# RG-LRU gate matmuls split into two 64-row halves of the array, in a hybrid RG-LRU / HGRN2 decoder layer on one Trainium2 core

## The reference

```python
xb = x.reshape(B, L, N_BLK_A, BLK_A)                       # 8 blocks of 64 channels
r = sigmoid(einsum('blnc,ncd->blnd', xb, wa).reshape(B, L, D_A) + ba)
i = sigmoid(einsum('blnc,ncd->blnd', xb, wx).reshape(B, L, D_A) + bx)
log_a = -C_RGLRU * softplus(-lam) * r
a = exp(log_a)
u = sqrt(maximum(-expm1(2.0 * log_a), 0.0)) * (i * x)
h = associative_scan over tokens of (a, u)                 # h[t] = a[t] * h[t-1] + u[t]
ya = h * silu(ga)
```

## Time and profile before

| | |
|---|---|
| time before, median of 3 runs | 1014.89 us (1014.86 to 1016.26) |
| the profiled execution: its own time, its span | 1015.58 us, 1013.8 us |
| PE busy | 965.2 us, 95% of the span |
| DVE, ACT, POOL busy | 585.0, 429.9, 161.9 us |
| mean granted TensorE clock | 0.984 of full |
| gate matmuls (L509), 128 records | 32.5 us busy, 399 ns mean |

### The profile page before, as it was taken

The page is one execution under the profiler, slowest core; times in us unless marked ns, Lnnn a source line. Parts: engine busy times, 40 slices in busy tenths (PEclk is TensorE's granted clock), DMA queues, the critical chain, the costliest instruction groups (busy, mean ns, idle before and its releaser), DMA issues.

```text
span 1013.8 us, 20053 instructions
## 1 busy us (share of the span) xinstructions
PE 965.2 (95%) x7447; PEld 710.2 (70%) x7502; DVE 585.0 (58%) x1652; ACT 429.9 (42%) x810; POOL 161.9 (16%) x214
## 2 busy tenths in 40 slices
PE   5799968999999999999999999999999999999987
PEld 2567856579766977587757976697659775887554
DVE  2455786446763666357643775466636763477445
ACT  2535476134732374136513471337413651346321
POOL 4000036111120113011201112011201130111112
PEclk9999988999999999999999999999999999999998
DMA  9985211100110011001100011001101010100413
GB/s 313 324 289 167 84 42 45 60 20 3 42 63 0 21 41 63 0 21 42 52 11 21 0 42 63 0 21 41 63 0 41 0 51 1 43 1 25 118 43 112
DMA packets 46590, 60.62 MB, mean 60 GB/s; under 512 B 2748, under 2 KB 40208, under 8 KB 46524
## 3 DMA queue, kind: packets, MB, share of 16 engines
q1 hardware_dynamic: 46524, 59.86, 17.8%
HBM read 48.90 MB, written 10.95 MB: 59 GB/s over the span
## 4 chain that ended last, share of the span: by engine, by line
PE 88%; DVE 5%; DMA 2%; issue 2%; ACT 2%; SPq 1%; DVEq 0%; ACTq 0%
PE ring L392 66%; PE lev L466 7%; PE aux L509 3%; PE okv L493 1%; PE lev L471 1%; PE okv L495 1%; PE okv L494 1%; PE lev L464 1%; DMA woh<-in_ada_w_dram 1%; DMA work<-in_w_in_dram 1%; PE okv L817 1%; PE aux L443 1%; PE aux L479 1%; PE aux L430 1%; PE okv L430 1%
## 5 line engine op out<-in xcount | busy, mean ns | idle before, releaser
L392 PE MATMUL ring<-hnh,wih 128*128 128x256 bf16 (+1 forms) x1152 | 289.4, 262 | 2.6 <-DVE hnl L1281 2.2
L392 PE MATMUL ring<-hnl,wih 128*128 128x256 f16 (+1 forms) x1152 | 289.6, 262 | 0.0
L392 PE MATMUL ring<-hnh,wil 128*128 128x256 bf16 (+1 forms) x1152 | 289.6, 262 | 0.0
L392 PE MATMUL ring<-woh,work 128*128 128x512 f16 x512 | 162.3, 379 | 1.6
L392 PEld LDWEIGHTS ring<-hnh,wih 128*128 128x128 f16 x1152 | 111.8, 99 | 15.1 <-issue 2.2
L1173 DVE TENSOR_TENSOR qq<-qq,gg 128x256 f32<-128x256 f32 x96 | 42.8, 446 | 133.6 <-PE lev L466 95.8
L392 PEld LDWEIGHTS ring<-hnl,wih 128*128 128x128 f16 x1152 | 109.9, 98 | 12.2
L392 PEld LDWEIGHTS ring<-hnh,wil 128*128 128x128 bf16 x1152 | 110.0, 98 | 11.9
L392 PE MATMUL ring<-wih,hnh 128*128 128x512 f16 (+1 forms) x264 | 101.2, 383 | 4.0 <-ACT kk L857 4.0
L392 PE MATMUL ring<-wih,hnl 128*128 128x512 f16 (+1 forms) x264 | 101.1, 383 | 1.4 <-issue 0.2
L1595 POOL TENSOR_TENSOR kk<-kk,cols 128x256 f32<-128x256 f32 x32 | 29.3, 935 | 410.7 <-ACT kk L857 410.7
(11 more groups left out here) (313 smaller groups left out, 1573.5 us busy)
## 6 DMA issues: line engine op xcount, KB each, us to landing
xin<-in_x_prompt_dram SPq DMA_DIRECT2D x16, 512.0 KB, 3.3
work<-in_x_prompt_dram SPq DMA_DIRECT2D x16, 512.0 KB, 4.1
out_dram<-work SPq DMA_DIRECT2D x16, 512.0 KB, 2.6
work<-in_ada_w_dram SPq DMA_DIRECT2D x4, 1024.0 KB, 10.4
woh<-in_ada_w_dram SPq DMA_DIRECT2D x4, 1024.0 KB, 11.8
work<-in_w_in_dram SPq DMA_DIRECT2D x4, 1024.0 KB, 8.5
woh<-in_w_in_dram SPq DMA_DIRECT2D x4, 1024.0 KB, 10.2
wol<-in_w_in_dram SPq DMA_DIRECT2D x4, 1024.0 KB, 9.5
```

Source lines behind the costliest of these rows:

```text
L392: last = mm(out, a(k), b(k), start=start and k == ks[0] and j == 0, stop=stop and k == ks[-1] and j == 2)
```

## The change

`wg` becomes `[128, 4, 128]`: for each channel tile, rows 0 to 63 hold `[wa | wx]` of the even block (columns 0 to 63 the r block, 64 to 127 the i block), rows 64 to 127 hold `[wx | wa]` of the odd block. There are no zeros left, so the memset on POOL and the waits for it go. `gates(n, p)` issues 4 matmuls as before, but each contracts over 64 rows only: half 0 writes `aux[0]`, half 1 writes `aux[1]`, and each result holds 64 channels of r and 64 channels of i. r comes out on its own partitions, i on the other half's. `gates_out` therefore needs 8 sigmoids of 64 partitions x 256 in place of 4 of 128 x 256, each behind one common signal `gates_done`. `r_sig` and `i_sig` count 8 per body.

Waits on PE move with it: both banks are written from the first matmul on, so `gates(n, p)` waits for `kt_sb` ahead of all four; `turn_y` waits for all sigmoids at once, and so does `turn_x`; the first projection of the next body waits for the first r sigmoid of pair 1 (`r_sig.at(n - 1, 5)`) where it waited for all i sigmoids.

```diff
-        wg = sb("wg", [P, 2, CT, P])
+        wg = sb("wg", [P, CT, P])
...
-        gr_ps, gi_ps = Signal("gr_ps", 2), Signal("gi_ps", 2)
+        gates_done = Signal("gates_done", 2)
...
-        r_sig, i_sig, a_exp, th_ok = (Signal(s, 4) for s in ("r_sig", "i_sig", "a_exp", "th_ok"))
+        r_sig, i_sig = Signal("r_sig", 8), Signal("i_sig", 8)
+        a_exp, th_ok = Signal("a_exp", 4), Signal("th_ok", 4)
...
                 if i == 6:
-                    sp.wait_ge(zeroed, 1)
                     for w, src in ((0, rg_wa), (1, rg_wx)):
                         for odd in range(2):
                             v = src[0].rearrange("(t two) c d -> two c t d", two=2)[odd]
-                            sp.dma_start(wg[64 * odd:64 * odd + 64, w, :, 64 * odd:64 * odd + 64], v).then_inc(wg_ld, 16)
+                            co = 64 * (w ^ odd)
+                            sp.dma_start(wg[64 * odd:64 * odd + 64, :, co:co + 64], v).then_inc(wg_ld, 16)
...
                 if j == 0:
                     pe.wait_ge(yb_ok.sem, yb_ok.at(n, 8))
-                    pe.wait_ge(r_sig.sem, r_sig.at(n, 4))
-                else:
-                    pe.wait_ge(i_sig.sem, i_sig.at(n, 4))
+                    pe.wait_ge(r_sig.sem, r_sig.at(n, 8))
+                    pe.wait_ge(i_sig.sem, i_sig.at(n, 8))
...
             def gates(n, p):
                 pe.wait_ge(cvc.sem, cvc.at(n, 8 * p + 8))
-                for w, s in ((0, gr_ps), (1, gi_ps)):
-                    if p == 0 and w == 0:
-                        if not isinstance(n, int) or n > 0:
-                            pe.wait_ge(ytl.sem, ytl.at(n - 1, 2))
-                    elif w == 1:
-                        pe.wait_ge(kt_sb.sem, kt_sb.at(n, p + 1))
-                    elif not (isinstance(n, int) and n == BODIES - 1):
-                        pe.wait_ge(hn_lo.sem, hn_lo.at(n + 1, 2))
-                    for c in range(2):
-                        last = mm(aux[(1 + w + p) % 2][:, T * c:T * c + T], wg[:, w, 2 * p + c, :], xc[:, c, :],
+                if p == 0:
+                    if not isinstance(n, int) or n > 0:
+                        pe.wait_ge(ytl.sem, ytl.at(n - 1, 2))
+                elif not (isinstance(n, int) and n == BODIES - 1):
+                    pe.wait_ge(hn_lo.sem, hn_lo.at(n + 1, 2))
+                pe.wait_ge(kt_sb.sem, kt_sb.at(n, p + 1))
+                for c in range(2):
+                    for half in range(2):
+                        rows = slice(64 * half, 64 * half + 64)
+                        last = mm(aux[half][:, T * c:T * c + T], wg[rows, 2 * p + c, :], xc[rows, c, :],
                                   start=True, stop=True)
-                    last.then_inc(s.sem, 1)
+                last.then_inc(gates_done.sem, 1)
...
                 weights(1)
                 if not first:
-                    pe.wait_ge(i_sig.sem, i_sig.at(n - 1, 4))
+                    pe.wait_ge(r_sig.sem, r_sig.at(n - 1, 5))
                 project(ring[0], FR, 0, n)
...
                 level(n, 1, 6)
-                pe.wait_ge(r_sig.sem, r_sig.at(n, 2))
+                pe.wait_ge(r_sig.sem, r_sig.at(n, 4))
+                pe.wait_ge(i_sig.sem, i_sig.at(n, 4))
                 if not last_body:
                     turn_x(n + 1, 0)
-                    pe.wait_ge(i_sig.sem, i_sig.at(n, 2))
                     turn_x(n + 1, 1)
...
-            pe.wait_ge(i_sig.sem, i_sig.at(n - 1, 4))
+            pe.wait_ge(i_sig.sem, i_sig.at(n - 1, 8))
...
-            for w in range(2):
-                for c in range(CT):
-                    o = TD * CT * w + TD * c
-                    last = mm(lev[1][:, o:o + TD], wg[:, w, c, :], xcd[:, TD * c:TD * c + TD], start=True, stop=True)
+            pe.wait_ge(dv("gp_sb"), 1)
+            for c in range(CT):
+                for half, bank in ((0, lev[1]), (1, okv[0])):
+                    rows = slice(64 * half, 64 * half + 64)
+                    last = mm(bank[:, TD * c:TD * c + TD], wg[rows, c, :], xcd[rows, TD * c:TD * c + TD],
+                              start=True, stop=True)
             last.then_inc(dv("gates_ps"), 1)
...
-                act.wait_ge(gr_ps.sem, gr_ps.at(n, p + 1))
+                act.wait_ge(gates_done.sem, gates_done.at(n, p + 1))
                 act.wait_ge(iu.sem, iu.at(n, p))
                 for c in range(2):
-                    A(rr[:, c, :], aux[(1 + p) % 2][:, T * c:T * c + T], ACT.Sigmoid,
-                      bias=pcol("ba", 2 * p + c)).then_inc(r_sig.sem, 1)
-                act.wait_ge(gi_ps.sem, gi_ps.at(n, p + 1))
+                    for half in range(2):
+                        at = slice(64 * half, 64 * half + 64)
+                        A(rr[at, c, :], aux[half][at, T * c:T * c + T], ACT.Sigmoid,
+                          bias=pcol("ba", 2 * p + c)[at, :]).then_inc(r_sig.sem, 1)
                 act.wait_ge(scan.sem, scan.at(n, 2 * p))
                 for c in range(2):
-                    A(ii[:, c, :], aux[p][:, T * c:T * c + T], ACT.Sigmoid, bias=pcol("bx", 2 * p + c)).then_inc(i_sig.sem, 1)
+                    for half in range(2):
+                        at, of = slice(64 * half, 64 * half + 64), slice(64 - 64 * half, 128 - 64 * half)
+                        A(ii[at, c, :], aux[half][of, T * c:T * c + T], ACT.Sigmoid,
+                          bias=pcol("bx", 2 * p + c)[at, :]).then_inc(i_sig.sem, 1)
```

More of the change, by code:

```diff
@@ L727, in _ @@
             pe.wait_ge(wg_ld, 64)
-            pe.wait_ge(zeroed, 3)
+            pe.wait_ge(zeroed, 2)
             pe.wait_ge(carry_zero, 2)
@@ L904, in gates_out @@
             def gates_out(n, p):
-                act.wait_ge(gr_ps.sem, gr_ps.at(n, p + 1))
+                act.wait_ge(gates_done.sem, gates_done.at(n, p + 1))
                 act.wait_ge(iu.sem, iu.at(n, p))
                 for c in range(2):
-                    A(rr[:, c, :], aux[(1 + p) % 2][:, T * c:T * c + T], ACT.Sigmoid,
-                      bias=pcol("ba", 2 * p + c)).then_inc(r_sig.sem, 1)
-                act.wait_ge(gi_ps.sem, gi_ps.at(n, p + 1))
+                    for half in range(2):
+                        at = slice(64 * half, 64 * half + 64)
+                        A(rr[at, c, :], aux[half][at, T * c:T * c + T], ACT.Sigmoid,
+                          bias=pcol("ba", 2 * p + c)[at, :]).then_inc(r_sig.sem, 1)
                 act.wait_ge(scan.sem, scan.at(n, 2 * p))
                 for c in range(2):
-                    A(ii[:, c, :], aux[p][:, T * c:T * c + T], ACT.Sigmoid, bias=pcol("bx", 2 * p + c)).then_inc(i_sig.sem, 1)
+                    for half in range(2):
+                        at, of = slice(64 * half, 64 * half + 64), slice(64 - 64 * half, 128 - 64 * half)
+                        A(ii[at, c, :], aux[half][of, T * c:T * c + T], ACT.Sigmoid,
+                          bias=pcol("bx", 2 * p + c)[at, :]).then_inc(i_sig.sem, 1)
             def decay(n, p):
-                act.wait_ge(r_sig.sem, r_sig.at(n, 2 * p + 2))
+                act.wait_ge(r_sig.sem, r_sig.at(n, 4 * p + 4))
                 for c in range(2):
@@ L1087, in _ @@
                 for c in range(CT):
-                    o = W4 * w + TD * c
-                    A(dst[:, TD * c:TD * c + TD], lev[1][:, o:o + TD], ACT.Sigmoid, bias=pcol(bias, c)).then_inc(dv("ri_d"), 1)
-            act.wait_ge(dv("ri_d"), 2 * CT)
+                    for half, bank in ((0, lev[1]), (1, okv[0])):
+                        at = slice(64 * half, 64 * half + 64)
+                        of = at if w == 0 else slice(64 - 64 * half, 128 - 64 * half)
+                        A(dst[at, TD * c:TD * c + TD], bank[of, TD * c:TD * c + TD], ACT.Sigmoid,
+                          bias=pcol(bias, c)[at, :]).then_inc(dv("ri_d"), 1)
+            act.wait_ge(dv("ri_d"), 4 * CT)
             for c in range(CT):
@@ L1445, in _ @@
             rest(2)
-            dve.wait_ge(zeroed, 3)
+            dve.wait_ge(zeroed, 2)
             body(0, True, False)
@@ L1524, in _ @@
             dve.wait_ge(dv("a_d"), 2 * CT)
-            dve.wait_ge(dv("ri_d"), 2 * CT)
+            dve.wait_ge(dv("ri_d"), 4 * CT)
             link(V.tensor_tensor(iid, iid, xcd, ALU.mult))
@@ L1612, in gated @@
             def gated(n, p):
-                pool.wait_ge(i_sig.sem, i_sig.at(n, 2 * p + 2))
+                pool.wait_ge(i_sig.sem, i_sig.at(n, 4 * p + 4))
                 G.tensor_tensor(ii[:, :, :], ii[:, :, :], xc[:, :, :], ALU.mult).then_inc(ix_ok.sem, 1)
@@ L1674, in _ @@
                 pool.wait_ge(gsum_ok, g + 1)
-            G.memset(wg[:, :, :, :], 0.0).then_inc(zeroed, 1)
             pool.wait_ge(ident_ok, 1)
```

## The result

| | before | changed |
|---|---|---|
| median of 6 runs | 1015.05 us | 1020.14 us (1018.41 to 1021.49) |
| profiled execution, span | 1013.8 us | 1018.2 us |
| PE busy | 965.2 us | 956.8 us |
| ACT busy | 429.9 us | 466.2 us |
| one loop body, start to start of `gates(n, 0)` | 108.43 us | 108.95 us |

The change makes the kernel slower: the ratio is 1.0049, with an interval of 1.0036 to 1.0062. The forecast was 1011.8 us, in a range of 1008.5 to 1016.0. In the changed kernel most lines are shifted by 1 to 10: the projections are L393, the sigmoids L912 and L918, the squares of `squares_o` L879, the products into `gbs` L1211.

The account below looks back on a forecast made before the run. PE was taken to bound the kernel, busy 108.13 us of a 108.5 us body. Terms -4.7 + 1.0 - 0.5 + 1.4 - 0.3 = -3.1 us took the median from 1014.89 to 1011.8 us, range 1008.5 to 1016.0.

Parts of the forecast that it names:

- first gates blocks, bodies 1 to 7: `gates(n, 0)`: PE has no wait there, so it gains 0.67 us each, 7 x -0.67 = -4.7 us.
- second gates blocks, bodies 1 to 6: `gates(n, 1)`: ACT's longer chain to `turn_y` takes PE's gain and costs 0.17 us each, +1.0 us.
- body 7's second block, up to the decode's first projection: Gain of 0.67 us less a 0.15 us wait for the i sigmoids: 0.5 us saved.
- the decode's gate matmuls: 16 records of 32 columns: -0.7 us if weight loads on the halves overlap, +0.2 if not; -0.3 taken.
- the rest of the decode: Eight more sigmoids, POOL's memset and the DMA's wait lie under other work: 0 us.
- body 0, up to `gates(1, 0)`: ACT's 1.46 us delay POOL's subtraction and then DVE: +1.4 us, bounds 0 and 2.
- step of 0.365 us: ACT's sigmoids: start-to-start distance taken as unchanged with half the partitions, so four more cost 1.46 us.
- sigmoids across halves that take longer: ACT's sigmoids: listed as something that would make the forecast wrong, with no size given.
- nil slack at `turn_y`: PE and the chain through ACT and DVE arrive together at `turn_y`; 0.05 us are lost there already.
- rival of five steps: Gates block: 8 records need five steps, 1.28 us, s = 0.45; total -1.3 us, 1013.6 us; chance 0.14.
- that of no overlap: Gates block: row halves don't overlap, 1.9 us, s = -0.20; total +4.6 us, 1019.5 us; chance 0.11.
- s: PE's saving per gates block: 1.73 us to 1.06 us, 0.67 us, counting 0.20 for two tiling switches.

Follow-up runs that it names:

- second profile: The changed kernel unaltered, profiled once more; body 108.94 us, `gates(1, 0)` starts at 245.72 us.
- e1: Kernel before, same full-array gate matmuls and old waits, each sigmoid split into two of 64 partitions; 1022.43 us, ratio 1.0080.
- e4: Changed kernel with sigmoids reordered in both groups: both column blocks of one half, then both of the other; 1014.63 us, ratio 1.0003.
- e7: e6 with sigmoids half by half, and the i sigmoids late in bodies 1 to 6 only; 1017.98 us, ratio 1.0030.
- e8: Changed kernel with sigmoids half by half; in bodies 1 to 6, pair 1's i sigmoids behind the squares and product ii*xc on DVE, not POOL; 1013.61 us.
- e5: Changed kernel with the old wait: the next body's first projection waits for all eight i sigmoids; 1019.14 us, ratio 1.0040.
- e6: e3 with POOL's pair 1 product ii*xc, from body 1 on, waiting for the eight products into `gbs`; 1022.93 us, ratio 1.0071.
- e9: Kernel before plus relaxed projection wait; in bodies 1 to 6, i sigmoids behind the squares and product on DVE; 1020.12 us, ratio 1.0048.
- e3: Changed kernel with pair 1's four i sigmoids moved behind `squares_o(n, 3)` in bodies 0 to 6; 1016.75 us, ratio 1.0015.
- e10: e8 with, in bodies 1 to 6, only two i sigmoids behind `squares_o(n, 3)`, two ahead, and POOL's aa*aa in its own buffer; 1011.61 us.

## Why the prediction was wrong

In the second profile, which has no stretch at the lower clock ahead of the first block, the forecast's terms compare as follows (span 1016.4, before 1013.8; its own time is 1018.13 us, still outside the range).

| term | forecast | measured |
|---|---|---|
| first gates blocks, bodies 1 to 7 | -4.7 | -4.3 (7 x 0.61) |
| second gates blocks, bodies 1 to 6 | +1.0 | +6.7 (6 x 1.12) |
| body 7's second block, up to the decode's first projection | -0.5 | +0.4 (6.10 us for 5.70) |
| the decode's gate matmuls | -0.3 | -0.8 (1.02 us for 1.80) |
| the rest of the decode | 0 | -1.3 (87.39 us for 88.68) |
| body 0, up to `gates(1, 0)` | +1.4 | +1.8 (245.72 for 243.94) |
| sum | -3.1 | +2.5 |

- **The step that failed is the length of a sigmoid's step.** "Their length doesn't follow the partitions" is right (470 ns for 64 partitions, 471 for 128). The step of 0.365 us drawn from it is not: 0.365 was read from sigmoids that all lie on the same partitions. In the order of the change each goes to the other half, and the step is 0.496. Eight of them are 1.05 us longer than reckoned, and at a place without slack all of it counts: 6 x 1.05 = 6.3 us. e1 and e4 show it. The prediction named this among the signs of being wrong ("sigmoids across halves that take longer"), but gave it no price.
- **The nil slack at `turn_y`, the chain and the place of the new wait were right.** L443's wait was forecast at about 0.9 a body and is 1.48; a second block was forecast to cost 0.17 and costs 1.12. Of the 0.95 between, the sigmoids are 1.05; the sigmoids start 2.31 us after the block in place of 2.42 (-0.11), the entry to the block (next point) adds 0.09, and from the squares to L443 it takes 5.75 us for the forecast 5.82 (-0.07).
- **PE's block was right at 1.06 us,** and with it that two halves run at once: inside the block two records start within 0.01 us of each other, in four pairs; the second pair starts 0.32 us after the first, the others 0.22 after the one before. The rival of five steps (1.28) and that of no overlap (1.9) are out. But the block's borders cost more than the 0.20 that I counted: the distance from the last projection matmul (597.09) to the block is 0.31 where 0.21 was, and at the end 598.46 to 598.79 is 0.33 where it was 0.22. So s is 0.67 - 0.20, about 0.46, in the second blocks. It is 0.61 in the first, where the 0.11 behind the block is missing and the block took 1.78 us before, not 1.73. The rival of five steps had s = 0.45, from the rule in the Trainium skill ("TensorE: Matmul & The Clock Gate", section The mechanism). That this number is near is luck. The starts do keep an order in the trace, but the two records of one matmul don't stand next to each other: the decode's alternate between `lev` and `okv` (the last section has them), and there is no fifth step.
- **Body 0 was right in kind:** the subtraction starts at 136.19, 2.2 us later than before, and 135.4 was forecast; in e4, with the faster order, it starts at 135.48. That the term of +1.8 is near +1.4 shows less: e7 and e8 differ by 2.3 us in a body 0 of one program, and e1, with the same slow sigmoids, had +0.1.
- **Body 7's second block failed by the same step.** PE waits 0.80 us for the i sigmoids, where 0.15 was reckoned, so the forecast gain of 0.5 us is a loss of 0.4. The decode's first projection in the second profile, 6.10 us after the start of the block (921.88):

```profile
927.97 0.18 PE L393 MATMUL ring<-hnh,wih 128*128 128x32 bf16 x1 [0.80 <-ACT ii L918]
```

- **The decode's gate matmuls were under-sized.** Their 16 records start in pairs 0.11 us apart and end the block after 1.02 us in place of 1.8: both weight loads and matmuls of the two halves overlap, the better bound of the two, -0.7.
- **The rest of the decode hid about 1 us of the loss by luck.** From the gate matmuls to the end it is 54.2 us before, 53.1 in the second profile, and 54.0 in e4, which has the changed kernel's decode. What differs is where a stretch at the lower clock falls: it covers 5.93 us of PE's work before, 3.67 in the second profile and 5.59 in e4, in this order:

```profile
984.80:991.60 6.80, 5.93 (x17) 2.42 (x18) 5.59 (x24) 0.00 (x0) 0.00 (x0) 0.50 0.13 51
```

```profile
986.20:993.00 6.80, 3.67 (x12) 1.60 (x13) 5.38 (x26) 0.00 (x0) 1.16 (x1) 0.50 0.00 1
```

```profile
983.40:990.20 6.80, 5.59 (x16) 2.29 (x17) 5.59 (x24) 0.00 (x0) 0.00 (x0) 0.50 0.07 30
```

- **The relaxed wait gives nothing,** as reckoned (e5).
- **The rivals.** None was the case that came. The price of +1 us that I gave the second blocks had a range for the step of 0.35 to 0.40, taken from one kind of sequence; the bound that was missing is a step without overlap, the instruction's own 0.47 to 0.48 us, which stands in the earlier trace rows as 0.84 - 0.365 = 0.475. By it eight sigmoids are 0.9 longer and the sum is 5 us more, 1017. The median of 1020.14 is 2 us above the second profile's execution; the first profile, at 1019.99, owes 1.6 to the stretch ahead of its first block, and how many of the six runs had one isn't known.

## What to carry to other kernels

Where an engine and a chain arrive together, the price per instruction of that chain must be bounded by its whole duration, not by the distance of starts in the best-packed sequence: neighbours that overlap by 0.11 us with one order and not at all with the other were worth 6 us here. If an activation must be split by partitions, issue all instructions of one half before the other; this exchange of two loops alone gave back 3.2 us in six bodies, and 5 in the medians. A faster block on the bound engine pays only if the chains that it meets next are shortened as well, and there were two of them: e6 and e9 relieved one at the other's cost, e3 ran into POOL's product, and only e10 relieved both.

## What the runs showed of the hardware

- Sigmoids of 256 columns on 64 partitions start 0.37 to 0.38 us apart on the same half and 0.48 to 0.50 when the half changes; each lasts 0.45 to 0.47 us. The i sigmoids of the changed kernel, which read from the other half of the partitions than they write, take 1.95 us for four, as those of e1, which don't.
- Two 64-row halves of the array run float32 matmuls side by side: 8 records of 256 columns in 1.06 us. Ahead of the block the distance of starts was 0.09 us longer than before the change, and behind it, into 128-column float32 matmuls, 0.11, on top of about 0.2 inside the block. Weight loads overlap as well; the decode's 32-column matmuls, in pairs on `lev` and `okv`:

```profile
964.37 0.27 PE L800 MATMUL lev<-xin,wg 64*128 64x32 f32 x1
964.38 0.27 PE L800 MATMUL okv<-xin,wg 64*128 64x32 f32 x1
964.48 0.27 PE L800 MATMUL lev<-xin,wg 64*128 64x32 f32 x1
964.49 0.27 PE L800 MATMUL okv<-xin,wg 64*128 64x32 f32 x1
```

- A DVE step over four numbers per partition took 1.12 us instead of 0.16 under a POOL product of 1.26 us.
- The changed kernel ran body 0 with and without a stretch at the lower clock between 121.5 and 125.5 us, and its two executions differ by 1.6 us at `gates(1, 0)` through this. In e7 and e8 one program of body 0 took 119.46 and 121.72 us at granted clocks of 0.81 and 0.73 from 140 to 185 us.
